# A hybrid encoder layer on one core: its tail in three passes (tile 0, dense tiles, tile 1) instead of two

## What is computed

```python
z = h @ w_in + b_in                      # Fourier | dilated q,k,v | memory q | 3 gates of 1024
y_a = fourier_mix(z_a) @ w_a             # 512 -> 1024
y_b = mixture_of_dilated_windows(qkv) @ w_b   # 256 -> 1024
y_c = attention_into_mem(q_c, mem) @ w_c # 512 -> 1024
merged = sum(sigmoid(gate_i) * y_i)
h = layer_norm(ALPHA * h + merged @ w_o)

q = (h @ w_pq).reshape(n_tok, 8, 2, 64)  # 8 heads, two halves
s1, s2 = q[:, :, 0] @ sub_keys1.T, q[:, :, 1] @ sub_keys2.T    # 128 keys each
v1, i1 = top_k(s1, 16); v2, i2 = top_k(s2, 16)
sc, ic = top_k(v1[..., None] + v2[..., None, :], 16)           # of 256 candidates
experts, gate = 128 * e1 + e2, softmax(sc)                     # 128 experts a token
y = sum_k gate_k * gelu(u_tab[expert_k] . h) * v_tab[expert_k]
h = layer_norm(ALPHA * h + y)
```

## Time and profile before

| | |
|---|---|
| median of 3 runs | 1941.82 us (1940.89 to 1942.91) |
| the profiled execution | 1940.42 us |
| its span in the profile | 1938.6 us |
| TensorE busy / weight loads / VectorE / ScalarE / POOL | 90% / 68% / 66% / 10% / 33% |
| moved by DMA | 493.88 MB, mean 255 GB/s |
| mean granted clock of TensorE | 0.947 |

### The profile page before, as it was taken

The page is one execution under the profiler, slowest core; times in us unless marked ns, Lnnn a source line. Parts: engine busy times, 40 slices in busy tenths (PEclk is TensorE's granted clock), DMA queues, the critical chain, the costliest instruction groups (busy, mean ns, idle before and its releaser), DMA issues.

```text
span 1938.6 us, 20568 instructions
## 1 busy us (share of the span) xinstructions
PE 1752.5 (90%) x7748; PEld 1324.9 (68%) x7748; DVE 1273.0 (66%) x2650; ACT 202.5 (10%) x422; POOL 640.3 (33%) x536
## 2 busy tenths in 40 slices
PE   7999999998999699999558899999999867899993
PEld 6588878887888578888457766666666567644441
DVE  3342184113065969994998877767876889876667
ACT  1101042000212021111100011101110100000000
POOL 1000000000023512223732377556566622475431
PEclk9999999999999889999877899999999977899997
DMA  6624201452388957777953399999999942599995
GB/s 215 228 66 136 81 2 59 150 170 94 126 264 310 387 193 249 238 253 287 393 179 96 124 402 409 409 409 409 394 409 409 409 152 66 174 410 409 409 406 207
DMA packets 193840, 493.88 MB, mean 255 GB/s; under 512 B 14104, under 2 KB 92953, under 8 KB 193445
## 3 DMA queue, kind: packets, MB, share of 16 engines
q0 software_dynamic: 74672, 271.55, 37.0%
q1 hardware_dynamic: 119068, 221.01, 31.9%
HBM read 489.32 MB, written 7.90 MB: 256 GB/s over the span
## 4 chain that ended last, share of the span: by engine, by line
PE 48%; DMA 19%; DVE 18%; POOL 8%; issue 6%; ACT 0%; SPq 0%; DVEq 0%; ACTq 0%
PE ps L615 47%; DMA arena<-in_v_tab_dram,experts 17%; DVE arena L1308 6%; POOL arena L580 4%; POOL arena L589 4%; DVE arena L1286 3%; DMA arena<-in_w_mem_kv_dram 1%; PE ps L627 1%; DMA arena<-in_u_cols_dram 1%; DVE i L1209 1%; DMA arena<-in_w_in_dram 1%; DVE arena L1275 1%; DVE pos L1224 1%; DVE v L1208 1%; DVE best L1223 1%
## 5 line engine op out<-in xcount | busy, mean ns | idle before, releaser
L615 PE MATMUL ps<-arena 128*128 128x256 f32 (+5 forms) x6272 | 1526.2, 406 | 100.6 <-DVE arena L1276 66.6
L615 PEld LDWEIGHTS ps<-arena 128*128 128x128 f32 (+2 forms) x6272 | 1116.8, 186 | 501.2 <-issue 254.5
L580 POOL DMA_INDIRECT arena<-in_u_tab_dram,experts x256 | 328.0, 1281 | 937.4 <-DVE dots L1286 540.3
L1308 DVE SCALAR_TENSOR_TENSOR arena<-arena,coef 128x1024 f32<-128x1024 f32 x254 | 326.9, 1287 | 95.8 <-DMA arena<-in_v_tab_dram,experts 94.9
L1286 DVE CUSTOM_DVE_ANT_0 arena<-arena 128x1024 f32<-128x1024 f32 x256 | 312.9, 1224 | 82.5 <-DMA arena<-in_u_tab_dram,experts 82.5
L589 POOL DMA_INDIRECT arena<-in_v_tab_dram,experts x256 | 301.1, 1176 | 141.8 <-DVE arena L1308 88.4
L865 ACT ACTIVATE arena<-ps 128x256 f32<-128x256 f32 (+1 forms) x204 | 87.9, 438 | 715.2 <-PE ps L615 660.4
L615 PE MATMUL ps<-hotg,arena 128*128 128x64 bf16 x768 | 99.0, 302 | 29.6 <-DVE hotg L1276 29.6
L615 PEld LDWEIGHTS ps<-hotg,arena 128*128 128x128 bf16 x768 | 91.9, 146 | 33.0 <-DVE hotg L1276 32.3
L1171 DVE TENSOR_TENSOR arena<-arena,ps 128x256 f32<-128x256 f32 x32 | 13.4, 420 | 124.9 <-PE ps L615 124.9
L865 ACT ACTIVATE arena<-ps,bT 128x256 f32<-128x256 f32 (+1 forms) x68 | 36.5, 537 | 350.9 <-PE ps L615 350.9
(11 more groups left out here) (129 smaller groups left out, 812.3 us busy)
## 6 DMA issues: line engine op xcount, KB each, us to landing
arena<-in_u_cols_dram SPq DMA_DIRECT2D x128, 512.0 KB, 6.7
arena<-in_v_tab_dram SPq DMA_DIRECT2D x128, 512.0 KB, 6.8
arena<-in_w_in_dram SPq DMA_DIRECT2D x37, 1024.0 KB, 5.4
arena<-in_w_o_dram SPq DMA_DIRECT2D x8, 1024.0 KB, 6.9
arena<-in_w_pq_dram SPq DMA_DIRECT2D x8, 1024.0 KB, 6.4
beta_copies<-beta_rows SPq DMA_DIRECT2D x1, 4608.0 KB
arena<-in_w_mem_kv_dram SPq DMA_DIRECT2D x4, 1024.0 KB, 19.0
arena<-in_w_a_dram SPq DMA_DIRECT2D x8, 512.0 KB, 5.2
```

What stands on the lines that cost most here:

```text
L580: nc.gpsimd.indirect_dma_start(out=u_ring[:, n % ROWS, :], out_offset=None, in_=u_tab[0], in_offset=bass.IndirectOffsetOnAxis(ap=experts[: ...
L615: return nc.tensor.matmul(dst, lhsT, rhs, start=start, stop=stop, skip_group_check=True)
L1308: nc.vector.scalar_tensor_tensor(out=y_acc, in0=row, scalar=by, in1=y_acc, op0=ALU.mult, op1=ALU.add).then_inc(v_used, 1)
```

## The change

The groups become three: tile 0, tiles 2 and 3, tile 1, so the tail is three passes, each over all weights of gates, branches, output and queries. Passes 0 and 2 have 128 moving columns in G, Yo and Q. The queries of pass 0 now follow the first 8 units of the dense pass, the dense queries the first 8 units of the last pass, and tile 1's queries come last. The norm of the two dense tiles is one joint call. Eight of the 16 dense selections stand between the branch units of the last pass (from the sixth on), the other eight after its norm. The pairs are dealt out anew: 38 in the dense pass, 12 over the last pass, 8 with the late selections, 32 after (24 ahead of the shares, 8 after the key transposes), 4 in the first one-hots, 115, 4, 64. The logits are split from `shares` and come ahead of the 24 pairs. SP waits for the last branch unit before it loads the u table. Buffers move: tile 0's attention output, `o_1` of three tiles, sigmoid and merge buffers of 256 columns, and the accumulator `y_acc` into tile 0's columns of `hT`, 8 pieces of 128 instead of 4 of 256.

```diff
-GROUPS = ((0, 1), (2, 3))
-GATHER = GROUPS[0]
-DENSE = GROUPS[1]
+GROUPS = ((0,), (2, 3), (1,))
+NORM_AT = {tile: n + 1 for n, tile in enumerate(tile for g in GROUPS for tile in g)}
+WIDTHS = tuple(len(tiles) * P for tiles in GROUPS)
+GATHER = (0, 1)
+DENSE = (2, 3)
...
-TAIL_PAIRS = 32
-TOP_PAIRS = DN
-REST_PAIRS = 26
-X_PAIRS = (10, 10)
-V_PAIRS = (112, PAIRS_IN - TAIL_PAIRS - TOP_PAIRS - REST_PAIRS - sum(X_PAIRS) - 112)
+TAIL_PAIRS = 38
+TOP_PAIRS = 20
+REST_PAIRS = 32
+X_PAIRS = (4, 4)
+V_PAIRS = (115, PAIRS_IN - TAIL_PAIRS - TOP_PAIRS - REST_PAIRS - sum(X_PAIRS) - 115)
 FIRST_TOPS = 6
 TAIL_UNITS = 32
+LAST_UNITS = 28
+TOPS_LATE = 8
...
 def tail_pairs(n):
 
-    return max(0, TAIL_PAIRS * (n - FIRST_TOPS) // (TAIL_UNITS - 1 - FIRST_TOPS))
+    if n < TAIL_UNITS:
+        return max(0, TAIL_PAIRS * (n - FIRST_TOPS) // (TAIL_UNITS - 1 - FIRST_TOPS))
+    return TAIL_PAIRS + (TOP_PAIRS - TOPS_LATE) * (n + 1 - TAIL_UNITS) // LAST_UNITS
...
-    first, second = gate_units(0), gate_units(1)
-    return (first + out_units(0) + second[:EARLY_NEXT] + query_units(0) + second[EARLY_NEXT:] + out_units(1)
-            + query_units(1))
+    out = gate_units(0) + out_units(0)
+    for g in range(1, len(GROUPS)):
+        later = gate_units(g)
+        out += later[:EARLY_NEXT] + query_units(g - 1) + later[EARLY_NEXT:] + out_units(g)
+    return out + query_units(len(GROUPS) - 1)
...
-        y_acc = hT[:, 4:8, 0:GW]
+        y_acc = hT[:, :, 0:P]
...
+            wait_full(sp, ("Yo", 2, DK - 1, 2))
+
             def u_table(e):
...
-                    product(key, bank(key, 0, GW), [(w[:, k, (j % 2) * P:(j % 2 + 1) * P], hT[:, k, toks])
-                                                    for k in range(DK)])
+                    product(key, bank(key, 0, WIDTHS[g]), [(w[:, k, (j % 2) * P:(j % 2 + 1) * P], hT[:, k, tokens(g)])
+                                                           for k in range(DK)])
...
-            top_pairs = lambda e: TAIL_PAIRS + min(TOP_PAIRS, e * 3 // 10)
+            top_pairs = lambda e: tail_pairs(TAIL_UNITS + LAST_UNITS - 1) + min(TOPS_LATE, e * TOPS_LATE // 24)
+            rest_pairs = lambda e: top_pairs(CW) + REST_PAIRS * max(0, e - 28) // (CW - 28)
...
                 table_acts(e)
                 after_pairs(top_pairs(e), top_pairs(e + 1))
-            after_pairs(top_pairs(CW), chunk_pairs(0))
+                after_pairs(rest_pairs(e), rest_pairs(e + 1))
...
             def first_norm(g):
-                for r, tile in enumerate(GROUPS[g]):
-                    wait_done(dve, ("WO", g, 3, r))
-                    layer_norm(h_tile, [tile], c, gain_in, 64, h1_ready)
+                wait_done(dve, ("WO", g, 3, len(GROUPS[g]) - 1))
+                layer_norm(h_tile, list(GROUPS[g]), c, gain_in, 64, h1_ready)
...
                 pairs(tail_pairs(n - 1) if n else 0, tail_pairs(n))
-            first_norm(1)
-            for i in range(DN):
+                if key == ("WO", 1, 3, len(GROUPS[1]) - 1):
+                    first_norm(1)
+            soon = DN - TOPS_LATE
+            for m, key in enumerate([key for key in dve_tail if key[1] == 2]):
+                tail_unit(key)
+                if key[0] == "Yo":
+                    lo, hi = (soon * max(0, m + i - 3) // (LAST_UNITS - 8) for i in range(2))
+                    for i in range(min(lo, soon), min(hi, soon)):
+                        top_halves(GN + i)
+                        top_pairs(GN + i)
+                n = TAIL_UNITS + m
+                pairs(tail_pairs(n - 1), tail_pairs(n))
+            first_norm(2)
+            for i in range(soon, DN):
                 top_halves(GN + i)
                 top_pairs(GN + i)
-                pairs(TAIL_PAIRS + i, TAIL_PAIRS + i + 1)
+                at = TAIL_PAIRS + TOP_PAIRS - DN + i
+                pairs(at, at + 1)
+            logits()
+            at = TAIL_PAIRS + TOP_PAIRS
+            pairs(at, at + REST_PAIRS * 3 // 4)
             shares()
-            pairs(TAIL_PAIRS + TOP_PAIRS, TAIL_PAIRS + TOP_PAIRS + REST_PAIRS // 2)
             for r in range(GT):
                 tail_unit(("ET", r))
-            pairs(TAIL_PAIRS + TOP_PAIRS + REST_PAIRS // 2, chunk_pairs(0))
+            pairs(at + REST_PAIRS * 3 // 4, chunk_pairs(0))
```

More of the change, by code:

```diff
@@ L137, in out_units @@
 def out_units(g):
-    return [(("WO", g, c, r), "dve") for c in range(4) for r in range(GT)]
+    return [(("WO", g, c, r), "dve") for c in range(4) for r in range(len(GROUPS[g]))]
 def query_units(g):
-    out = [(("h1T", g, r, q), "act") for r in range(GT) for q in range(2)]
+    out = [(("h1T", tile, q), "act") for tile in GROUPS[g] for q in range(2)]
     for n in range(HEADS):
@@ L236, in chunk_of @@
     what, g = key[0:2]
+    if what == "h1T":
+        return None
     if what == "G":
@@ L738, in tail_unit @@
                 what, g = key[0:2]
-                lo = place(g) if what != "ET" else 0
-                toks = slice(lo, lo + GW)
                 if what == "G":
@@ L749, in tail_unit @@
                     at_o, n = ((0, 4), (4, 2), (6, 4))[b]
-                    product(key, bank(key, 0, GW), [(w[:, k, (j % 2) * P:(j % 2 + 1) * P], o[g][:, at_o + k, :])
-                                                    for k in range(n)])
+                    product(key, bank(key, 0, WIDTHS[g]), [(w[:, k, (j % 2) * P:(j % 2 + 1) * P], o[g][:, at_o + k, :])
+                                                           for k in range(n)])
                 elif what == "WO":
@@ L774, in tail_unit @@
                     begin(key)
-                    for r in range(GT):
+                    for r in range(len(GROUPS[g])):
                         last = mm(bank(key, r * 2 * KEYS, (r + 1) * 2 * KEYS), query(g, n)[:, r * P:(r + 1) * P],
@@ L911, in tail_unit @@
                     n = 2 * GA[0] + 8 * b + j
[L912 removed]
+                    take(key, sig[:, at_n % SIGS, 0:WIDTHS[g]], bank(key, 0, WIDTHS[g]), ACT.Sigmoid, bias=bT[:, n:n + 1])
                 elif what == "h1T":
[L914 to L915 removed]
+                    tile, q = key[1:]
                     take(key, hT[:, 4 * q:4 * q + 4, tile * P:(tile + 1) * P], quads(bank(key)))
@@ L922, in tail_unit @@
                         wait_full(sca, ("SC", g - 1, HEADS - 2 + n))
-                    take(key, query(g, n), bank(key, 0, GW))
+                    take(key, query(g, n), bank(key, 0, WIDTHS[g]))
                 elif what == "SC":
                     n = key[2]
-                    take(key, scores[g].rearrange("p (r n) k -> p r n k", r=GT)[:, :, n, :],
-                         bank(key).rearrange("p (r k) -> p r k", r=GT))
+                    if g == 1:
+                        take(key, scores[1].rearrange("p (r n) k -> p r n k", r=GT)[:, :, n, :],
+                             bank(key).rearrange("p (r k) -> p r k", r=GT))
+                    else:
+                        take(key, scores[0][:, g // 2 * HEADS + n, :], bank(key, 0, 2 * KEYS))
             def gates_of(s):
@@ L1245, in top_pairs, with logits @@
                                                    ).then_inc(expert_ready, 1)
-            def shares():
+            def logits():
                 mine = slice(GN, STEPS)
@@ L1253, in shares @@
                                         ).then_inc(logits_ready, 1)
+            def shares():
+                mine = slice(GN, STEPS)
                 dve.wait_ge(exps_ready, 1)
```

75 lines of the change are left out of this document (36 added, 39 removed).

## The result

The changed kernel takes **1963.12 us** (median of 4 runs, 1961.06 to 1968.62) beside 1941.36 for the kernel before (4 runs, 1940.41 to 1942.91): a ratio of 1.0115, 95% interval [1.0102, 1.0128]. It is slower by 21.8 us. The profiled execution took 1961.79 us with a span of 1960.0, 21.4 over the one before; the forecast for that difference was +13.5, and 1963 lies inside the range 1929 to 1980.

What follows compares the result with a forecast made beforehand. The end was set by when the one-hots begin plus the row pairs then left. First dot +67.3, key transposes to one-hots -14.7, the rest -39.1 gave +13.5 us on 1940.4 profiled: median 1955, range 1929 to 1980.

Steps and rivals of the forecast that it cites:

- Theory A: Last pass: selections among its branch units chain the table dots to VectorE; 1944 to 1967 us, chance 0.60.
- Narrow records: TensorE at 128 columns: 0.116 us a record, 0.232 a matmul, 7% over half the wide price.
- rival D: Narrow records pay for their weight loads, 0.154 us each, 29 us more: 1984 us, chance 0.06.
- norm of the dense tiles, 19.0 us: Between dense output projection and dense queries: output take, two pairs, joint norm, transposes; 22.7 us before, so -3.7 us.
- eight early units: First units of the last pass, 10.2 us of matmuls, taken to lie inside the dense tiles' norm.
- The dense pass: Second pass, 38 pairs for 32: more rows on the DMA, less a little for a moved selection; +7 us.
- 9.2 us stall: Dense pass: a stall made by the first burst of gathered rows, kept in the sum.
- rival B: Faster: ring keeps up in the dense pass, burst stall and added 7 us vanish, records 0.109 us; 1934 us, chance 0.17.
- Rival C: Slower still: weight ring starves both early passes, +11 and +8 us over the forecast; 1974 us, chance 0.13.
- Tile 0's pass: First pass, now 128 columns: cheaper gates, branches and output units, 1 us charged for strips; -67.1 us.
- the last pass: New work between the dense queries and the first table dot, VectorE's 95.8 us against 52.9 of matmuls; +148.3 us.
- some 40 us stall: Last pass: TensorE's wait for the last branch unit ahead of the output projection.

Runs made afterwards that it cites:

- 3: Changed kernel with all 16 dense selections behind the last pass's norm, the 8 pairs spread over them and ScalarE's part over 40 dots; 1938.44 us.
- 5: Changed kernel with 5 selections in the last pass instead of 8, late pairs spread over 11, last 8 pairs ahead of the key transposes; 1927.43 us, again 1925.21.
- 1: Changed kernel with its last 8 row pairs and the selection among them moved from behind the key transposes to ahead of them; 1944.37 us.
- Experiment 11: Kernel of 5 with 26 pairs spread over the dense pass and 13 placed where the dense queries run; 1914.39 us.
- 8: Kernel before with the new dealing of pairs, and ScalarE's exponentials ahead of dot 42 instead of 48; 1945.21 us.
- 9: Kernel of 8 with ScalarE's activations of the later pairs among dots 50 to 63 instead of behind the last dot; 1936.48 us.
- 10: Changed kernel with 32 pairs in the dense pass instead of 38, the 6 put into the first table sums; 1973.00 us.
- 4: Kernel before, still two passes, with the new dealing of pairs alone; 1945.36 us.
- 7: Changed kernel with 10 of the last pass's 12 pairs at its start, in VectorE's wait for the dense queries; 1953.00 us.
- experiment 6: Kernel of 3 with the 12 row pairs of the last pass also moved behind its norm; one run, 1959.26 us.

## Why the prediction was right

**The direction and the main mechanism held.** Theory A, the forecast, was that the dots begin later because the last pass is chained to VectorE. Its prices came out: VectorE busy 87.9 us in the stretch priced at 95.8 of VectorE's work, and 96.4 us in all for the 100.4 (4.6+95.8) forecast; norm and queries behind it 49.4 against 47.9; its waits 31.65, 21.4 and 42.3 us for the 30, 20 and 45 forecast. Experiments 3 and 5 remove this chain in part and gain; 1 removes what the wait of 42 us held up and gains 18.8.

**Narrow records.** 0.112 us against my 0.116; rival D (0.154) fell. The Trainium skill's spacing of 81 ns at 128 columns beside a formula of 56 ("TensorE: Matmul & The Clock Gate", Back-to-back issue gap) does not carry over as a ratio: half of the 0.216 us at 256 columns is 0.108, and the record is 4% above that, not 45%.

**The step that failed** is the term "norm of the dense tiles, 19.0 us": it took 31.1, and these 12.1 us are more than the whole error of 7.9. I had given VectorE one output unit and two pairs between the last output matmul and the norm, 5.1 us; it had four pairs at 3.4 us, slowed by their rows, and needed 13.3. The norm itself came out (10.9 us for 11.2). The other 4 us are strips. I priced eight early units by their matmuls and put them inside VectorE's norm, "inside it" meaning hidden; their strips were issued just when the gathers had the DMA, TensorE waited 3.35 and 10.40 us for them, and the early units ended 4.0 us after the norm. Experiment 11, with 12 pairs fewer in the dense pass, bears out both: VectorE starts the norm 11.9 us after the output projection although an 8 us selection now stands among its units, the strips' wait is 4.9 us, and the dense queries begin 3.0 us after the norm's end instead of 6.7.

**A term that came out by luck.** The dense pass was forecast at +7 and measured at +8.5, but not for the reason given. I took the 12 rows more as time on the DMA, and thought that the selection which leaves the output units would save a little. It went ahead of the last branch unit instead, and TensorE waited 13.08 us for that unit; its waits for DMA in the pass were 1.9 us. The "9.2 us stall" of the first burst, kept in the sum and taken off in rival B, was no stall either: the earlier trace rows gives the time that a strip took to land, and TensorE's wait for it in the kernel before is the 0.61 us of this row.

```profile
557.11 69.33 PE L615 MATMUL ps<-arena 128*128 128x256 f32 x320 [0.61 <-DMA arena<-in_w_in_dram]
```

Rival C named starved rings and put them in the wrong places: the pass of tile 0, where no wait is above 0.75 us at a DMA share of 0.89, did not starve.

**Smaller ones.** The dots took 4.1 us more, 2.8 of them for table columns that come late (TensorE waits 5.1 us for them, 2.3 before). Tile 0's pass gained 3 us more than forecast, the last pass 2.5, the one-hot stages 5.0; the sums and the end gave 3.2 less. All terms but the norm together take 4 us off its 12.1: that the total is within 8 us is in part their cancelling.

**Where the experiments' own forecasts failed.** For 3, 8, 9 and 10 I took a wait away and booked its length. In 3 the second limit of the last pass, its strips, stood at 78 us beside the 96: of the forecast's "some 40 us stall" only 18 were the selections'. In 4 the pairs brought a stall of TensorE that I had not looked for, and in 8 and 9 the next wait of the same engine, or of the engine behind it, took most of what the last had given. In 10 selections moved into the last pass and the one-hots. Where the next limit was worked out as well (5, 7 and 11, which took the last pass's second limit from 3) the medians came 14, 7 and 6 us from the forecasts, against 14, 14, 11 and 20 for these four: better, and still off where a second wait was missed.

**Open.** Whether a fourth slot in the strip ring would take the 8 us of waits that experiment 6 leaves, or the late strips at the head of the last pass, was not tried. Nor was the changed kernel with 38 pairs and only its selection moved behind the last branch unit, which would price the 13.08 us alone. Why the new dealing gains less in the two-group kernel than the chain of its waits suggests is settled only as far as 9 goes, with ScalarE's order as the suspect.

## What to carry to other kernels

Before booking a wait as gain, find the second limit of the same stretch (other engine, DMA ring) and the next wait of the same engine; the smaller difference is the gain. In an order written out by hand, a long piece of work must not stand just ahead of the unit that the next stage waits for (a selection of 8 us there made a stall of 13), and work that needs nothing must not stand behind a wait; a split by share (three quarters ahead, one quarter behind) is worth checking first: here one line was 19 us of 22. When a pass is moved, price its first loads against what is in the queues at that moment, not against their landing time in a quiet stretch.

## What the runs showed of the hardware

**Strips against gathered rows.** A 1 MB strip landed in 5.4 us in the pass of tile 0, beside no gathers (the median of nine), and in 21.9 us beside rows that hold 76% of the DMA. In those 32 us the rows' queue moved 2631 packets for 9.55 MB and the strips' 2989 for 3.00 MB; at the same place in experiment 10 it was 2532 for 9.25 MB and 2545 for 2.55 MB. So the two queues got about as many packets each, and with rows of 4 KB against 1 KB the strips got a quarter of the bytes. That the engines take turns by packet would explain it; no run here varies the row length.

**Strips of 1 KB cost DMA share.** Tile 0's pass used a share of 0.89 for 286 GB/s, which is 321 at full share (its fullest 6 us, 360 GB/s at 1.07, give 336); the table sums reach 400 at 1.01. That stands against the Trainium skill's rule that transfers from 512 B run at line rate ("DMA: Bandwidth & Descriptors", Specifications). The forecast's 314 GB/s, from rows of before, was near, and no wait above 0.75 us came of it at 0.89.

**An fp32 matmul** of 128 columns costs 0.224 us in its two records and one of 256 columns 0.432: two narrow ones are 4% dearer than one wide, although every weight is loaded twice as often (the load, 0.112 us a record in the same stretch at 57.32 us for 512, keeps step with the matmuls instead of adding to them).
